# Hybrid encoder step on one core: square sums of the input norm regrouped, pooled products from split operands, two last chunks on GpSimd

## The chip, the cores and the metric

One core of one Trainium2 chip runs the program. The metric is device time in microseconds (us). Before the change three runs gave 808.74, 809.33 and 810.02 us; the median, 809.33 us, is the time before. One more execution was profiled: it took 807.98 us, and its span from the first to the last instruction is 806.0 us.

## The reference, cut to what matters

The reference computes one layer for 16 meta rows, 512 prompt rows and 64 sample rows (592 rows of 1024 numbers). All of it is float32. The parts that the change touches:

```
hp = layer_norm(concat(meta, x_prompt), ln_in_g, ln_in_b); hs = layer_norm(x_sample, ...)   # input norm
z = h @ w_in + b_in                      # split into u, q, k, v, ga, gb
pooled = trailing means of u over 2, 4, 8, 16 rows, minus u      # one window for each group of 128 columns
pool_out = einsum('btgc,gcd->btgd', pooled, w_pool_grp) * pool_scale   # four 128x128 products
attn = stick_breaking_attention(q, keys, vals)
mix = sigmoid(ga) * (pool_out @ w_br_pool) + sigmoid(gb) * (attn @ w_br_attn)
h = layer_norm(ALPHA * h + mix @ w_out + b_out)
f = square(relu(h @ w_mlp1 + b_mlp1)) @ w_mlp2 + b_mlp2
y = layer_norm(ALPHA * h + f, ln2_g, ln2_b)              # last norm, then the output
```

## The kernel before, in words

Activations stand transposed: 128 features on the partitions, eight chunks (k = 0 to 7) for the 1024 features, and the rows along the free axis, in two halves of 296 columns in the first stage. A float32 product is mostly made as three float32r products: each operand x is split into hi = x rounded to float32r and lo = x - hi, and TensorE adds hi*hi, lo*hi and hi*lo in PSUM. ScalarE makes the hi parts and VectorE the lo parts, of weights (units of 128x1024 from one stream) and of activations. Where a product is small it is left as a plain float32 matmul, which the trace shows as two instructions.

Each engine runs its own list of instructions in written order; semaphores tie the lists together. Nothing is reordered at run time, so an instruction that waits holds everything behind it on its engine.

**Input norm and keys (0 to 50 us).** x arrives in eight transfers. TensorE sums the columns with matrices of 1/1024 (`half1_sum`, `square_sum`), VectorE subtracts the mean (`centre0`), ScalarE squares (`square0`) and takes the inverse root (`root0`, a Ln, an Exp and a Square) and VectorE finishes it (`inverse0`). Then, chunk by chunk: VectorE scales (`scale0`, line 1953), ScalarE adds the bias and rounds (`norm0_hi`, line 1282), VectorE makes the rest (`norm0_lo`, line 1959), and TensorE multiplies the chunk into two key units at a time (`keys_pair`, lines 737 to 740): the second unit of the pair runs `lag` chunks behind the first, and an optional function is called between chunks. There are four such passes: units 0, 1 and units 2, 3 on the first half of the columns (half 0), then both pairs on half 1. In the first pass the lag is 1 and after each chunk one square sum of half 1 is taken (line 706); in the three others the lag is 4. Weights of units 2 and 3 are split inside this stage (`split_keys`, lines 1288 and 1966). The results leave PSUM by `key_out` on ScalarE (line 1295), and the next pass waits for that: unit 1 on half 1 needs the bank that `key_out(3, 0)` frees.

**Attention and fillers (75 to 300 us).** Eleven items of attention. In each TensorE makes scores, ScalarE and VectorE turn them into softplus sums and split these (`sums_hi`, `sums_lo`, the latter line 2063), TensorE takes suffix sums (line 866), ScalarE exponentiates, TensorE multiplies by the values. While TensorE waits for the softplus sums it does halves of linear units from the stream. GpSimd meanwhile makes the pooled frames (lines 2660 to 2671, until 176 us) and then issues a small store. The four products of the pooled prompt frames with `w_pool_grp` (`pool_group`, line 937) are plain float32 matmuls of 512 columns, after items 6, 7 and 8 and inside item 9; VectorE scales each (`pool_scale`) back into `u_t`. A fifth call does the 64 sample columns.

**Last norm (780 to 806 us).** The columns are in two parts of 320 and 256. For the second part, after the last product, ScalarE, VectorE and TensorE make the mean and the inverse root (lines 1758 to 1769, 2503 to 2522), VectorE and GpSimd centre four chunks each (lines 2513, 2752), then for k = 0 to 7 VectorE scales (`scale2`, line 2533), ScalarE adds the bias (`norm2_out`, line 1775), and the SP queue stores chunks 0-1, 2-3, 4-5, 6 and 7 as they are ready (line 605). The kernel ends when the stores have landed.

Of the kernel before, what the change touches and what calls it, by code (L numbers as in the profile page):

```python
# [5 lines left out]
F32 = mybir.dt.float32  # L6
F32R = mybir.dt.float32r
BF16 = mybir.dt.bfloat16
ALU = mybir.AluOpType
# [147 lines left out]
def encoder_step(nc, x, wstream, w2_d, vecs_d, bv_d, kc_d, vc_d, state_d, wpool_d, y_out, k_out, v_out, s_out):  # L157
    with ExitStack() as ctx:
# [47 lines left out]


# [95 lines left out]
        win_done, ust_done, pooled = sem("win_done"), sem("ust_done"), sem("pooled")  # L303
        pool_mm, pool_scaled, pool_hi_done, pool_lo_done = (
# [27 lines left out]
        n2_last_mean = sem("n2_last_mean")  # L332
# [90 lines left out]
        BY_DVE2 = (4, 4)  # L423

# [118 lines left out]
        def _(sp):  # L543
# [56 lines left out]
            for p, c in enumerate(PARTS2):  # L600

                for ks in ([slice(k, k + 2) for k in range(0, KC - 2, 2)] + [slice(k, k + 1) for k in range(KC - 2, KC)]
                           if p == LAST2 else [slice(k, k + 1) for k in range(KC)]):
                    sp.wait_ge(n2_out, KC * p + ks.stop)
                    sp.dma_start(y_out[:, ks, c], r2[:, ks, c]).then_inc(y_stored, 16)
            sp.wait_ge(y_stored, 16 * (2 * KC - 3))
# [6 lines left out]
        def _(pe):  # L613
# [154 lines left out]


            keys_pair(0, 0, square_sum1, 1)  # L770
            keys_pair(2, 0)
            keys_pair(0, 1)
# [156 lines left out]
            def pool_group(s):  # L929

                pe.wait_ge(pooled, 1)
                pe.wait_ge(wpool_in, 16)
# [3 lines left out]
                if s < 4:  # L936
                    pe.matmul(small[:, :], wpool[:, s, :], u_t[:, s, META:UP], start=True, stop=True)\
                        .then_inc(pool_mm, 1)
# [238 lines left out]
        def _(act):  # L1177
# [127 lines left out]
            root0(0)  # L1305
            act.wait_ge(vecs_in, 16)
            norm0_hi(0, 0)
            for k in range(1, KC):
                norm0_hi(k, 0)
                square0(k - 1, 1)  # L1310
                if k in (4, 6):
                    split_keys(k // 2)
            square0(7, 1)
            key_out(0, 0)
            root0(1)
            key_out(1, 0)
# [486 lines left out]
            for k in range(KC):  # L1803
                norm2_out(k, LAST2)


        @block.vector
        def _(dve):
# [168 lines left out]
            for k in range(1, KC):  # L1977
                scale0(k, 0)
                norm0_lo(k - 1, 0)
                centre0(k - 1, 1)  # L1980
            norm0_lo(7, 0)
            centre0(7, 1)

            dve.wait_ge(lo_split, 2)
            split_keys(2)
            split_keys(3)
            inverse0(1)
# [587 lines left out]
            for k in range(KC):  # L2575
                scale2(k, LAST2)

        @block.gpsimd
        def _(pool):
# [114 lines left out]
            pool.wait_ge(pooled, 1)  # L2694
# [117 lines left out]
```

## Time and profile before

| | |
|---|---|
| median of three runs | 809.33 us |
| profiled execution | 807.98 us, span 806.0 us |
| TensorE busy | 793.0 us (98% of the span) |
| VectorE busy | 506.4 us (63%) |
| ScalarE busy | 392.3 us (49%) |
| GpSimd busy | 101.8 us (13%) |
| chain of waits | TensorE 97%, ScalarE 1%, VectorE 1%, transfers 1% |

A timeline row gives the start in us from the span's beginning, the duration, the engine (PE is TensorE, DVE VectorE, ACT ScalarE, POOL GpSimd, SP the queue that issues transfers), the line of the kernel, the operation, output<-inputs with shapes, the count where neighbours of one kind are merged, and in brackets the idle time before it and who ended it. Matmuls overlap, so their spacing and not their duration is their price. Rows of the windows view give a stretch, its length, each engine's busy time and instruction count, the TensorE clock as a share, the share of the transfer engines and GB/s.

### The profile page before, as it was taken

What the parts mean: (1) busy time and instruction counts of PE and PEld (TensorE: products, weight loads), DVE (VectorE), ACT (ScalarE), POOL (GpSimd) and SP (SyncE); (2) the same over time, 40 slices, a digit from 0 to 9 for tenths busy, and PEclk for the clock granted to TensorE, in tenths of its full rate; (3) what the DMA queues carried; (4) which work ended last, traced back from release to release, by engine and by line L of the source; (5) the groups of instructions that cost most, each with busy time, mean ns of one, the idle gap of its engine ahead of it and who ended that gap; (6) DMA issues with size and microseconds to landing.
All of it is one profiled execution on the core that took longest, in us unless ns stands there. A gap on an engine that the chain in (4) does not pass through costs nothing.

```text
span 806.0 us, 14543 instructions
## 1 busy us (share of the span) xinstructions
PE 793.0 (98%) x5880; PEld 765.2 (95%) x5880; DVE 506.4 (63%) x858; ACT 392.3 (49%) x654; POOL 101.8 (13%) x120
## 2 busy tenths in 40 slices
PE   8999999999999999999999999999999999999995
PEld 6999899998988999999999999999999999999994
DVE  5823444753536376876877779775667887445645
ACT  4623345654646475562556663334554433344324
POOL 2100000570000000007720000000000000000355
PEclk9999999999999999999999999999999999999998
DMA  8732131112111112243302214222221423222203
GB/s 297 264 130 97 53 113 53 54 56 79 53 54 53 53 58 74 79 131 106 92 14 79 66 39 158 79 105 79 82 72 55 157 79 105 80 78 80 79 1 117
DMA packets 23033, 71.61 MB, mean 89 GB/s; under 512 B 2416, under 2 KB 6656, under 8 KB 22592
## 3 DMA queue, kind: packets, MB, share of 16 engines
q1 hardware_dynamic: 22288, 68.23, 25.7%
q0 software_dynamic: 544, 2.52, 0.9%
q8 instruction: 40, 0.66, 0.3%
q14 instruction: 17, 0.14, 0.1%
q10 hardware_dynamic: 144, 0.07, 0.1%
HBM read 65.96 MB, written 4.85 MB: 88 GB/s over the span
## 4 chain that ended last, share of the span: by engine, by line
PE 97%; ACT 1%; DVE 1%; DMA 1%; issue 0%; SPq 0%; ACTq 0%; DVEq 0%
PE lin L620 15%; PE lin L621 15%; PE lin L622 15%; PE z L1093 6%; PE z L1095 5%; PE z L1096 5%; PE z L866 3%; PE lin L996 3%; PE lin L997 3%; PE lin L998 3%; PE lin L1114 2%; PE lin L1113 2%; PE lin L1112 2%; PE z L925 1%; PE lin L740 1%; PE lin L737 1%
## 5 line engine op out<-in xcount | busy, mean ns | idle before, releaser
L620 PE MATMUL lin<-h_hi,whi 128*128 128x288 f32 (+1 forms) x832 | 247.3, 297 | 0.0
L621 PE MATMUL lin<-h_lo,whi 128*128 128x288 f32 (+1 forms) x832 | 245.9, 296 | 0.0
L622 PE MATMUL lin<-h_hi,wlo 128*128 128x288 f32 (+1 forms) x832 | 245.0, 294 | 0.0
L622 PEld LDWEIGHTS lin<-h_hi,wlo 128*128 128x128 f32 x832 | 156.6, 188 | 0.0
L620 PEld LDWEIGHTS lin<-h_hi,whi 128*128 128x128 f32 x832 | 156.5, 188 | 0.1
L621 PEld LDWEIGHTS lin<-h_lo,whi 128*128 128x128 f32 x832 | 156.4, 188 | 0.1
L1815 DVE TENSOR_TENSOR wlo<-raw,whi 128x1024 fp32r<-128x1024 f32 x65 | 80.3, 1235 | 34.8 <-ACT whi L1187 30.0
L1187 ACT ACTIVATE whi<-raw 128x1024 fp32r<-128x1024 f32 x58 | 60.9, 1051 | 50.3 <-PE lin L622 32.4
L1605 ACT ACTIVATE relu_t<-lin,vecs 128x288 f32<-128x288 f32 x60 | 30.1, 501 | 91.4 <-PE lin L622 88.0
L2257 DVE TENSOR_TENSOR relu_sq<-relu_t 128x288 f32<-128x288 f32 x60 | 27.5, 458 | 64.4 <-ACT relu_t L1605 64.4
L1093 PE MATMUL z<-f_ops,whi 128*128 128x288 f32 x216 | 64.0, 296 | 0.0
L1095 PE MATMUL z<-f_ops,whi 128*128 128x288 f32 x216 | 63.3, 293 | 0.0
L1096 PE MATMUL z<-f_ops,wlo 128*128 128x288 f32 x216 | 63.2, 293 | 0.0
L1652 ACT ACTIVATE whi<-w_set 128x768 fp32r<-128x768 f32 x36 | 30.5, 846 | 52.0 <-PE z L1096 41.7
L2732 POOL TENSOR_TENSOR sum<-r 128x576 f32<-128x576 f32 x1 | 1.4, 1435 | 346.4 <-DVE r L2497 346.4
L1093 PEld LDWEIGHTS z<-f_ops,whi 128*128 128x128 f32 x216 | 40.6, 188 | 0.4 <-issue 0.4
L2404 DVE TENSOR_TENSOR wlo<-w_set,whi 128x768 fp32r<-128x768 f32 x36 | 34.5, 957 | 9.9 <-ACT whi L1652 9.8
L1096 PEld LDWEIGHTS z<-f_ops,wlo 128*128 128x128 f32 x216 | 40.6, 188 | 0.0
L1095 PEld LDWEIGHTS z<-f_ops,whi 128*128 128x128 f32 x216 | 40.5, 188 | 0.0
L2034 DVE SCALAR_TENSOR_TENSOR sa<-z,sa 128x512 f32<-128x512 f32 (+4 forms) x25 | 19.8, 794 | 26.8 <-ACT sa L1363 26.8
L1095 PE MATMUL z<-f_ops,third_hi 128*128 128x288 f32 x120 | 35.6, 297 | 0.0
L1096 PE MATMUL z<-f_ops,third_lo 128*128 128x288 f32 x120 | 35.4, 295 | 0.0
(348 smaller groups left out, 1900.3 us busy)
## 6 DMA issues: line engine op xcount, KB each, us to landing
raw<-w_stream SPq DMA_DIRECT2D x88, 512.0 KB, 3.5
w_set<-w_sets SPq DMA_DIRECT2D x32, 384.0 KB, 3.6
r<-x_t SPq DMA_DIRECT2D x8, 296.0 KB, 5.1
kcache<-k_cache SPq DMA_DIRECT2D x1, 2048.0 KB, 9.0
vcache<-v_cache SPq DMA_DIRECT2D x1, 2048.0 KB, 10.7
y<-r SPq DMA_DIRECT2D x8, 160.0 KB, 1.8
k_new<-k_t POOLq DMA_DIRECT2D x1, 1184.0 KB, 4.8
v_new<-v_t POOLq DMA_DIRECT2D x1, 1024.0 KB, 5.2
```

The costliest lines, as they stand in the source:

```text
L620: pe.matmul(out, w_h, hi, start=first, stop=False)
L621: pe.matmul(out, w_h, lo, start=False, stop=False)
L622: return pe.matmul(out, w_l, hi, start=False, stop=last)
L1093: pe.matmul(out, w_h, f_op(f, i, 0), start=opens and i == 0, stop=False, skip_group_check=True)
L1095: pe.matmul(out, w_h, f_op(f, i, 1), start=False, stop=False, skip_group_check=True)
L1096: last = pe.matmul(out, w_l, f_op(f, i, 0), start=False, stop=i == PRS - 1, skip_group_check=True)
L1187: nc.scalar.activation(whi[:, j % SPLIT, :], raw[:, j, :], ACT.Copy).then_inc(hi_split, 1)
L1605: nc.scalar.activation(dst, lin[:, bank, 0:HA], ACT.Relu, bias=vec(V_B1 + u)).then_inc(bank_free[bank], 1)
L1652: nc.scalar.activation(op_home(o)[0], w_set[g % 2][:, i, :], ACT.Copy).then_inc(s_hi, 1)
L1815: tt(wlo[:, j % SPLIT, :], raw[:, j, :], whi[:, j % SPLIT, :].bitcast(F32), ALU.subtract)\
L2257: tt(dst, src, src, ALU.mult).then_inc(f_sq_done, 1)
L2404: tt(home[1], w_set[g % 2][:, RAW_SLOT[q], :], home[0].bitcast(F32), ALU.subtract).then_inc(s_lo, 1)
```

## The change

Three separate edits:

- **Input norm.** ScalarE's and VectorE's lists are reordered: in the first pass they no longer centre and square half 1 between the chunks of half 0; units 2 and 3 are split at other places; centring and squaring come afterwards, in two batches on VectorE. TensorE takes the eight square sums in the second pass, two after chunk 2 and six after chunk 3 of unit 2, with unit 3 a full eight chunks behind. In the third pass the lag is 2 instead of 4.
- **Pooled products.** GpSimd splits `w_pool_grp` (one pair of instructions on 512 columns) and each of the four pooled groups (a pair on 512 columns each) into hi and lo; the lo parts take the place of the frames. The rounding of groups 2 and 3 waits for the products of groups 0 and 1, because `u_hi` has two slots. TensorE's float32 matmul becomes three float32r ones.
- **Last chunks.** VectorE copies the inverse root from PSUM to SBUF and then scales only chunks 0 to 5; GpSimd scales chunks 6 and 7 and applies weight and bias. SP stores 0-1, 2-3 and 6-7; ScalarE issues the store of 4-5 itself.

```diff
 PE
-            keys_pair(0, 0, square_sum1, 1)
-            keys_pair(2, 0)
-            keys_pair(0, 1)
+            def square_sums1(k):
+                for n in {1: (0, 1), 2: range(2, KC)}.get(k, ()):
+                    square_sum1(n)
+            keys_pair(0, 0, None, 1)
+            keys_pair(2, 0, square_sums1, KC)
+            keys_pair(0, 1, None, 2)
             keys_pair(2, 1)
...
-                pe.wait_ge(pooled, 1)
-                pe.wait_ge(wpool_in, 16)
+                pe.wait_ge(wp_lo_done, 1)
...
-                    pe.matmul(small[:, :], wpool[:, s, :], u_t[:, s, META:UP], start=True, stop=True)\
-                        .then_inc(pool_mm, 1)
+                    pe.wait_ge(u_lo_done, s + 1)
+                    hi, lo = u_hi[:, s % 2, :], u_lo[:, s, META:UP]
+                    pe.matmul(small[:, :], wp_hi[:, s, :], hi, start=True, stop=False)
+                    pe.matmul(small[:, :], wp_lo[:, s, :], hi, start=False, stop=False)
+                    pe.matmul(small[:, :], wp_hi[:, s, :], lo, start=False, stop=True).then_inc(pool_mm, 1)
 ACT
             root0(0)
+            split_keys(2)
             act.wait_ge(vecs_in, 16)
-            norm0_hi(0, 0)
-            for k in range(1, KC):
+            for k in range(KC):
                 norm0_hi(k, 0)
-                square0(k - 1, 1)
-                if k in (4, 6):
-                    split_keys(k // 2)
-            square0(7, 1)
+            split_keys(3)
             key_out(0, 0)
+            for k in range(2):
+                square0(k, 1)
+            key_out(1, 0)
+            for k in range(2, KC):
+                square0(k, 1)
             root0(1)
-            key_out(1, 0)
...
-            for k in range(KC):
+            for k in range(G_FROM2):
                 norm2_out(k, LAST2)
+            act.wait_ge(n2_out, KC * LAST2 + G_FROM2)
+            act.dma_start(y_out[:, G_FROM2 - 2:G_FROM2, PARTS2[LAST2]], r2[:, G_FROM2 - 2:G_FROM2, PARTS2[LAST2]])\
+                .then_inc(y_stored, 16)
 DVE
                 scale0(k, 0)
                 norm0_lo(k - 1, 0)
-                centre0(k - 1, 1)
             norm0_lo(7, 0)
-            centre0(7, 1)
             dve.wait_ge(lo_split, 2)
             split_keys(2)
+            for k in range(4):
+                centre0(k, 1)
             split_keys(3)
+            for k in range(4, KC):
+                centre0(k, 1)
             inverse0(1)
...
-            for k in range(KC):
+            nc.vector.tensor_scalar(rstd2[:, PARTS2[LAST2]], r2_rstd(LAST2), 1.0, None, ALU.mult)\
+                .then_inc(n2_rstd_copy, 1)
+            for k in range(G_FROM2):
                 scale2(k, LAST2)
 POOL
             pool.wait_ge(pooled, 1)
+            pool.wait_ge(wpool_in, 16)
+            pool.wait_ge(qk_done, 3)
+            nc.gpsimd.tensor_scalar(wp_hi[:, :, :], wpool[:, :, :], 1.0, 0.0, ALU.mult, ALU.add).then_inc(wp_hi_done, 1)
+            pool.wait_ge(wp_hi_done, 1)
+            nc.gpsimd.tensor_tensor(wp_lo[:, :, :], wpool[:, :, :], wp_hi[:, :, :].bitcast(F32), ALU.subtract)\
+                .then_inc(wp_lo_done, 1)
+            for s in range(4):
+                if s >= 2:
+                    pool.wait_ge(pool_mm, s - 1)
+                nc.gpsimd.tensor_scalar(u_hi[:, s % 2, :], u_t[:, s, META:UP], 1.0, 0.0, ALU.mult, ALU.add)\
+                    .then_inc(u_hi_done, 1)
+                pool.wait_ge(u_hi_done, s + 1)
+                nc.gpsimd.tensor_tensor(u_lo[:, s, META:UP], u_t[:, s, META:UP], u_hi[:, s % 2, :].bitcast(F32),
+                                        ALU.subtract).then_inc(u_lo_done, 1)
...
             centre2(LAST2)
+            pool.wait_ge(n2_rstd_copy, 1)
+            for k in range(G_FROM2, KC):
+                c = PARTS2[LAST2]
+                pool.wait_ge(n2_centred_g, KC * LAST2 - sum(BY_DVE2) + k + 1)
+                nc.gpsimd.tensor_tensor(r2[:, k, c], r2[:, k, c], rstd2[:, c], ALU.mult).then_inc(n2_scaled_g, 1)
+                pool.wait_ge(n2_scaled_g, k - G_FROM2 + 1)
+                nc.gpsimd.tensor_scalar(r2[:, k, c], r2[:, k, c], vec(V_LN2_G + k), vec(V_LN2_B + k), ALU.mult, ALU.add)\
+                    .then_inc(n2_out_g, 1)
 SP (last part of the columns)
-                for ks in ([slice(k, k + 2) for k in range(0, KC - 2, 2)] + [slice(k, k + 1) for k in range(KC - 2, KC)]
-                           if p == LAST2 else [slice(k, k + 1) for k in range(KC)]):
-                    sp.wait_ge(n2_out, KC * p + ks.stop)
-                    sp.dma_start(y_out[:, ks, c], r2[:, ks, c]).then_inc(y_stored, 16)
+            for k in (0, 2, G_FROM2):
+                if k < G_FROM2:
+                    sp.wait_ge(n2_out, KC * LAST2 + k + 2)
+                else:
+                    sp.wait_ge(n2_out_g, KC - G_FROM2)
+                sp.dma_start(y_out[:, k:k + 2, PARTS2[LAST2]], r2[:, k:k + 2, PARTS2[LAST2]]).then_inc(y_stored, 16)
```

## Rows read from the trace of the kernel before

**Rows 1.** Page, section 1: busy us, share of the span, instructions.

```profile
PE 793.0 (98%) x5880; PEld 765.2 (95%) x5880; DVE 506.4 (63%) x858; ACT 392.3 (49%) x654; POOL 101.8 (13%) x120
```

**Rows 2.** Timeline, TensorE, pass of units 2, 3 and start of half 1.

```profile
31.86 0.37 PE L737 MATMUL lin<-h_hi,k_hi 128*128 128x296 f32 x1
...
36.40 0.30 PE L737 MATMUL lin<-h_hi,whi 128*128 128x296 f32 x1
```

**Rows 3.** Timeline, VectorE and ScalarE, 17 to 36 us, in two lists.

```profile
17.71 0.53 DVE L1959 SCALAR_TENSOR_TENSOR h_lo<-r,vecs,h_hi 128x296 fp32r<-128x296 f32 x1 [0.24 <-ACT h_hi L1282]
...
27.86 2.35 DVE L1966 TENSOR_TENSOR k_lo<-raw,k_hi 128x1024 fp32r<-128x1024 f32 x2
...
34.42 0.52 DVE L1959 SCALAR_TENSOR_TENSOR h_lo<-r,vecs,h_hi 128x296 fp32r<-128x296 f32 x1
34.86 0.52 DVE L1953 SCALAR_TENSOR_TENSOR r<-r,vecs,small 128x296 f32<-128x296 f32 x1
...
17.14 0.97 ACT L1282 ACTIVATE h_hi<-r,vecs 128x296 fp32r<-128x296 f32 x2 [1.67 <-DVE r L1953]
...
29.89 0.51 ACT L1273 ACTIVATE rstd<-z,eps 128x296 f32<-128x296 f32 x1 [1.06 <-PE z L706]
...
31.27 0.49 ACT L1295 ACTIVATE k_t<-lin,vecs 128x296 f32<-128x296 f32 x1
...
34.97 0.99 ACT L1282 ACTIVATE h_hi<-r,vecs 128x296 fp32r<-128x296 f32 x2
```

**Rows 4.** Chain of waits: start us, us added to the chain, what, count.

```profile
29.35 0.50 PE z L706 x2
...
80.86 0.24 PE small L791
...
222.39 1.06 PE small L937 x2
```

**Rows 5.** Timeline, GpSimd, VectorE, TensorE, 150 to 187 us, in three lists.

```profile
152.33 0.70 POOL L2665 TENSOR_SCALAR win<-win 128x591 f32<-128x591 f32 x1
...
169.43 1.19 POOL L2660 TENSOR_TENSOR win<-win 128x600 f32<-128x600 f32 x1
...
175.97 0.62 POOL L2678 DMA_DIRECT2D state_new<-ust  x1
...
170.27 1.43 DVE L1815 TENSOR_TENSOR wlo<-raw,whi 128x1024 fp32r<-128x1024 f32 x1 [0.63 <-ACT whi L1187]
...
176.17 0.99 DVE L2029 TENSOR_TENSOR sa<-sa 128x800 f32<-128x800 f32 x1
177.08 0.98 DVE L2063 TENSOR_TENSOR sp_lo<-sa,sp_hi 128x800 fp32r<-128x800 f32 x1
178.29 1.23 DVE L2063 TENSOR_TENSOR sp_lo<-sa,sp_hi 128x1024 fp32r<-128x1024 f32 x1 [0.23 <-ACT sp_hi L1395]
...
181.46 0.68 DVE L2121 TENSOR_TENSOR q_lo<-q_t,q_hi 128x512 fp32r<-128x512 f32 x1
...
178.48 0.34 PE L866 MATMUL z<-sp_hi,tri_r 128*128 128x400 f32 x1
...
179.71 0.39 PE L866 MATMUL z<-sp_hi,tri_r 128*128 128x512 f32 x1
...
186.30 0.39 PE L847 MATMUL z<-q_hi,k_hi 64*128 64x272 f32 x2
```

**Rows 6.** Timeline, the last norm's second part, 796 to 804 us.

```profile
796.87 2.77 POOL L2752 TENSOR_TENSOR r<-r,mean 128x256 f32<-128x256 f32 x4 [3.31 <-ACT mean L1759]
797.10 0.43 DVE L2506 TENSOR_SCALAR z<-z 128x256 f32<-128x256 f32 x1
...
800.33 3.30 ACT L1775 ACTIVATE r<-r,vecs 128x256 f32<-128x256 f32 x8 [1.48 <-DVE r L2533]
```

**Rows 7.** Windows of 0.2 us in the last stores; columns as told above.

```profile
802.80:803.00 0.20, 0.00 (x0) 0.00 (x0) 0.20 (x1) 0.20 (x2) 0.00 (x0) 0.50 0.53 174
...
805.00:805.20 0.20, 0.00 (x0) 0.00 (x0) 0.00 (x0) 0.00 (x0) 0.00 (x0) 0.50 0.93 323
```

More of the change, by code:

```diff
@@ L204, in encoder_step @@
         inv_d = sb("inv_d", [P], F32, A0 + 32832)
+        u_hi = sb("u_hi", [2, SEQ], F32R, A0 + 31480)
+        u_lo = sb("u_lo", [4, UT], F32R, A0 + 23360)
+        wp_hi, wp_lo = sb("wp_hi", [4, P], F32R, 17664), sb("wp_lo", [4, P], F32R, A0 + 13632)
         KQ = 3 * P
@@ L303, in encoder_step @@
         win_done, ust_done, pooled = sem("win_done"), sem("ust_done"), sem("pooled")
+        wp_hi_done, wp_lo_done, u_hi_done, u_lo_done = (
+            sem("wp_hi_done"), sem("wp_lo_done"), sem("u_hi_done"), sem("u_lo_done"))
         pool_mm, pool_scaled, pool_hi_done, pool_lo_done = (
@@ L331, in encoder_step @@
         n2_sq, n2_sum, n2_sumsq = ([sem(f"{n}{p}") for p in range(2)] for n in ("n2_sq", "n2_sum", "n2_sumsq"))
-        n2_last_mean = sem("n2_last_mean")
+        n2_last_mean, n2_rstd_copy, n2_scaled_g, n2_out_g = (
+            sem("n2_last_mean"), sem("n2_rstd_copy"), sem("n2_scaled_g"), sem("n2_out_g"))
         n2_msq, n2_mean, n2_var, n2_guess, n2_rstd = (
@@ L423, in encoder_step @@
         BY_DVE2 = (4, 4)
+        G_FROM2 = 6
         SUMMED2 = (KC, KC - 1)
@@ L599, in _ @@
                         load_unit(q4, j)
-            for p, c in enumerate(PARTS2):
-                for ks in ([slice(k, k + 2) for k in range(0, KC - 2, 2)] + [slice(k, k + 1) for k in range(KC - 2, KC)]
-                           if p == LAST2 else [slice(k, k + 1) for k in range(KC)]):
-                    sp.wait_ge(n2_out, KC * p + ks.stop)
-                    sp.dma_start(y_out[:, ks, c], r2[:, ks, c]).then_inc(y_stored, 16)
-            sp.wait_ge(y_stored, 16 * (2 * KC - 3))
+            for k in range(KC):
+                sp.wait_ge(n2_out, k + 1)
+                sp.dma_start(y_out[:, k, PARTS2[0]], r2[:, k, PARTS2[0]]).then_inc(y_stored, 16)
+            for k in (0, 2, G_FROM2):
[4 more added lines that the diff above has]
+                sp.dma_start(y_out[:, k:k + 2, PARTS2[LAST2]], r2[:, k:k + 2, PARTS2[LAST2]]).then_inc(y_stored, 16)
+            sp.wait_ge(y_stored, 16 * (KC + 4))
             sp.wait_ge(k_stored, 16)
@@ L1305, in _ @@
             root0(0)
+            split_keys(2)
             act.wait_ge(vecs_in, 16)
-            norm0_hi(0, 0)
-            for k in range(1, KC):
+            for k in range(KC):
                 norm0_hi(k, 0)
-                square0(k - 1, 1)
-                if k in (4, 6):
-                    split_keys(k // 2)
-            square0(7, 1)
+            split_keys(3)
             key_out(0, 0)
+            for k in range(2):
[3 more added lines that the diff above has]
+                square0(k, 1)
             root0(1)
-            key_out(1, 0)
             norm0_hi(0, 1)
```

## The prediction, made before the changed kernel ran

> **What bounds the kernel now.** I read the busy shares first: TensorE is busy 793.0 of 806.0 us [rows 1]. Nearly all of the 13 us that it is not lie at the two ends, before the first keys and in the last norm's tail. So the middle is paid by TensorE's work alone: what is taken off its list there shortens the time one to one, as long as no other engine becomes late for it, and a wait put into it lengthens the time one to one. At the two ends the waits count instead. So the timelines of the three places decide, and in each the reader should look for the operation that TensorE (or the last store) would wait for, and how long before its use it is ready.
>
> **The change, part by part.**
>
> **Input norm.** TensorE's own work is the same: 96 matmuls of 296 columns on half 0 and eight square sums at 0.50 us [rows 4]. Between 31.86 and 36.40 lie 33 matmuls, 0.137 us each [rows 2]. Only waits can go. Now the first pass is paced by TensorE with the square sums between the chunks, after a start that VectorE holds up. The last square sum ends at 29.85 (29.35 + 0.50) [rows 4], and half 1 starts at 36.40 [rows 2].
>
> After the change VectorE has only scale and rest for each chunk, 0.44 us apart between 34.42 and 34.86 [rows 3], 0.87 a chunk. The first rest still starts at 17.71 [rows 3]. Six chunks on is 22.93; the eighth rest waits for ScalarE's rounding and starts near 23.6. Then comes the lo split of unit 2: two of them took 2.35 [rows 3], so one ends about 1.2 after its start at 24.05, at 25.3. TensorE, which has 6 x 0.137 = 0.82 of work a chunk, follows VectorE's pace of 0.87 and is done at the same moment. So unit 2 starts at 25.3 and its first result is there 0.4 later (a matmul that restarts takes 0.37, [rows 2]), at 25.7; eleven more and eight square sums (11 x 0.137 + 8 x 0.50 = 5.5) end at 31.2. The squares themselves are in time: VectorE and ScalarE need until about 29.9 for the last. From 31.2, 36 matmuls (4.9) lead to half 1, at 36.1 where the end of the matmul before 36.40 was 36.56. That is 0.4 us gained. It costs nothing that ScalarE splits unit 2 ahead of the first rounding: it is idle there for 1.67 us before 17.14 [rows 3], and a split on it takes about 1.
>
> Then it is given back. Half 1's chain hangs on the last square sum, which now ends 1.35 later while TensorE has 0.4 less to do before it wants half 1. In the profile the root starts at 29.89, the scale of chunk 3 at 34.86, 5.0 after the sum [rows 3]. ScalarE rounds chunk 3 some 0.55 after that and can start the next operation 0.43 later, since a pair of roundings takes 0.99 [rows 3]. That next one is the eviction of unit 3, which frees the bank of unit 1; it takes 0.49 [rows 3]. It ends 6.5 after the last sum, and TensorE's first result on that bank comes 0.47 later (eviction at 31.27 + 0.49, next matmul 31.86 + 0.37) [rows 2, 3], at 6.95. With lag 2 TensorE wants that bank after 36 + 9 matmuls, so the 46th would end 46 x 0.137 = 6.3 after the sum. The wait is 0.65; behind it stand the rest of both units and everything after. Nothing later in half 1 waits. Net: 0.65 - 0.4 = **0.2 us lost**. Bounds: 0.4 gained if that eviction comes in time, 0.5 lost if the square sums also end some 0.3 late.
>
> **Pooled products.** A float32 product of 512 columns costs 1.06 us on the chain (one of four such rows) [rows 4]. A float32r one of 512 columns costs 0.24 [rows 4], three 0.71. Four groups: 4 x 0.35 = 1.4 us less for TensorE. The operands are ready long before: products start at 222, GpSimd is free from 176.
>
> But GpSimd's new work is not free at its start. GpSimd's store issue ends at 175.97 + 0.62 = 176.59 [rows 5], where VectorE is making the lo parts of item 4's softplus sums. Those are needed at once: the two end at 178.06 and 179.52, and TensorE uses them at 178.48 and 179.71 [rows 5], 0.4 and 0.2 us later. Where GpSimd and a VectorE operation with two inputs in SBUF meet, one stands still: a GpSimd addition runs from 169.43 to 170.62, and the VectorE subtraction of 1024 columns that starts at 170.27 ends at 171.70, taking 1.43 where the same shape takes 1.23 [rows 5]. It ended 1.08 after GpSimd: its own length less 0.15. With that, and taking turns: VectorE's sum holds until 177.16; the rounding (0.70 for 591 columns [rows 5], 0.61 for 512) ends at 177.62; the first lo part (0.98) ends at 178.45, just in time; the subtraction (1.19 for 600 columns, 1.02 for 512) ends at 179.32; the second lo part ends at 180.40, not 179.52. TensorE wants it at 179.71 and restarts about 0.1 late: **0.8 us of waiting**. Bounds: none, if VectorE keeps its place, and 1.4 if each blocked operation starts from nothing. Nothing makes up for it, since TensorE has no idle time afterwards. Net 1.4 - 0.8 = **0.6 us gained**, between 1.4 gained and nothing.
>
> The Trainium skill, page "SBUF — State Buffer", section "SBUF: two separate sides", says that the port pair which VectorE and GpSimd share is an exclusive lock for a whole instruction, and that the loser blocks fully. By that rule nothing overlaps, the 0.15 goes, the two lo parts end at 178.75 and 181.0, TensorE loses about 1.4, and the whole change comes out at 0.4 us slower instead of 0.2 faster; that lies inside the forecast's own range, and the 170.27 row speaks for the small overlap.
>
> The pairs for groups 2 and 3 run behind the products of groups 0 and 1, near 223 and 238, with more than 20 us to spare and no softplus work beside them. The fill of `ones_r` behind them moves by 60 us and is not needed before the output product near 300.
>
> **Last chunks.** VectorE's copy (0.43 for the like of it [rows 6], a little less in step) delays chunk 0's scale, ScalarE's output and the first store by 0.4. ScalarE writes six chunks, not eight, at 0.40 each (3.30 for eight with overlap [rows 6]), so its last output comes 0.8 - 0.4 = 0.4 earlier. GpSimd's four instructions at no more than 0.69 each (2.77 for four [rows 6]) from 800.2 end by 803.0, and its store is out before the transfers of 0-3 are through. If issue set the end, 0.4 would be gained. But the transfers do: from the first packet to 805.2 the engines are full (0.93 and more) save for two gaps of about a tenth, one at 802.8 [rows 7]. A megabyte that starts 0.4 later and at best closes the gaps ends **0.2 us later**. Bounds: 0.4 gained, 0.4 lost.
>
> **Sum.** +0.2 - 0.6 + 0.2 = -0.2 us on the profiled execution's 807.98, so 807.8. The median of the runs stands 1.35 above that execution; with it the forecast is **809.1 us**. Changes below 0.2% (1.6 us) can't be told from none with this kernel.
>
> **The rivals.**
>
> *No collision (chance 0.20).* GpSimd's first subtraction falls beside ScalarE's part or VectorE keeps the port, and the 1.4 stays whole: -1.4 + 0.2 + 0.2 = -1.0, 808.3 us. For it: the slack and the collision are both tenths of a microsecond. Against it: GpSimd is free at exactly the wrong time, and the 170.27 row shows VectorE losing.
>
> *All three pay (0.15).* No collision, no wait for the eviction in half 1 (the 0.4 stays), and the last store sets the end (another 0.4): -2.2, 807.1 us. For it: ScalarE's list does end earlier. Against it: each needs a row read the other way.
>
> *The collision goes on (0.08), the slower side.* GpSimd has four more instructions before it must wait, and VectorE then owes the lo split of a weight unit, `k_lo` and `q_lo`; `q_lo` ends at 182.14 and item 5's scores use it at 186.30 [rows 5]. With 0.9 lost already and four turns (two of 0.46, two of 0.87, together 2.7) it ends at 185.7, against scores moved to 187.1. It decides from 4.1 us of loss on; every further microsecond is one of the kernel, and with turns twice as long TensorE loses about 2: 811.0 us.
>
> *The three products cost what one did (0.07).* Weight loads that show would eat the 0.35 a group; then only the losses stay: +1.2, 810.5 us. Against it: rows of three float32r products in a row at 0.24.
>
> **How the numbers follow.** The forecast's own case has 0.50, with its own range of 808.4 to 809.9. Faster by over 0.2%: the 0.15 and a little of the first rival, 0.19. Slower: 0.08 and a little of the last, 0.10. The rest, 0.71, is no change. The range reaches from the middle of the all-pay case to the edge of the collision that goes on: 807.3 to 810.3.
>
> **What would show it.** Right: a wait of TensorE of about 0.65 before the first matmul of unit 1 on half 1, with the eviction of unit 3 just before it; VectorE's 1024-column lo part near 179 ending some 0.9 later than now against TensorE's list, and TensorE idle there; three float32r matmuls per group in 0.71; full transfer engines until the end. Wrong: TensorE without idle time between 20 and 790 us, a gain at the start that lasts to 50 us, or a gap in the transfers before the last store.

## The result, and the profile after

The changed kernel takes 810.11 us (median of 22 runs, 808.87 to 812.40); the kernel before took 809.28 us in the 22 runs beside them. The ratio, which is not that of the two medians (they lie 0.83 apart), is 1.0013 with a 95% interval of 1.0007 to 1.0019: 1.05 us slower, 0.6 to 1.5. The forecast was 0.2 us faster. The profiled execution took 808.87 us, span 807.1 us. One run of all that are told of below, 858.31 us at a granted clock of 0.849 with the best version, is a slow one and left out of ratios and spreads.

The busy times hardly show it. TensorE's share, from the page of the changed kernel:

```profile
PE 792.2 (98%) x5883; PEld 764.7 (95%) x5884; DVE 509.3 (63%) x857; ACT 391.6 (49%) x652; POOL 115.7 (14%) x134
```

It has 0.8 us less to do than before [rows 1] in a span 1.1 us longer. So it waits more, and the question is where. I set each product of TensorE against the same product in the trace of before; the table gives the start after minus the start before, in us, at some times of the trace of before. A step between two columns is a gain or a loss in that stretch.

| | first key product | 50 | 170 | 200 | 275 | 362 | 375 | 480 | 600 | 700 | 785 |
|---|---|---|---|---|---|---|---|---|---|---|---|
| changed kernel | -0.23 | 0.0 | 0.0 | 1.62 | 0.98 | 0.98 | 1.50 | 1.47 | 0.87 | 0.87 | 0.87 |

Six steps: the execution reached its first key product 0.23 earlier; +0.23 in the input norm; +1.62 between 176 and 182; -0.64 at the four pooled products; +0.52 at 367; -0.60 between 495 and 550. The last one is not the change's: further down it is in half of the kernels, whatever they hold.

*Input norm.* The timeline of the changed kernel where unit 1 begins on half 1, TensorE's products and the eviction of unit 3 on ScalarE:

```profile
36.69 0.30 PE L752 MATMUL lin<-h_hi,wlo 128*128 128x296 f32 x1
...
37.04 0.40 PE L754 MATMUL lin<-h_lo,whi 128*128 128x296 f32 x1
...
37.62 0.38 PE L751 MATMUL lin<-h_hi,whi 128*128 128x296 f32 x1 [0.18 <-issue]
...
37.03 0.49 ACT L1316 ACTIVATE k_t<-lin,vecs 128x296 f32<-128x296 f32 x1
```

Products here are 0.137 us apart [rows 2]. Between the first two rows it is 0.35, so 0.21 of waiting (the low part of chunk 2), and between the next two 0.58, so 0.44 (the bank that the eviction frees): 0.65 in all, against 0.43 gained at the start of half 1. That start is 18.15 us after the first key product, 35.74 - 17.59, where it was 36.40 - 17.82 = 18.58 [rows 2]; 35.74, 17.59 and 17.82 are starts of TensorE's products in the two traces.

*Collision.* GpSimd, VectorE and TensorE of the changed kernel where GpSimd begins to split:

```profile
176.63 1.42 POOL L2728 TENSOR_SCALAR wp_hi<-wpool 128x512 fp32r<-128x512 f32 x1
...
178.13 1.90 POOL L2730 TENSOR_TENSOR wp_lo<-wpool,wp_hi 128x512 fp32r<-128x512 f32 x1
...
180.01 1.59 POOL L2735 TENSOR_SCALAR u_hi<-u_t 128x512 fp32r<-128x512 f32 x1
...
181.68 2.15 POOL L2738 TENSOR_TENSOR u_lo<-u_t,u_hi 128x512 fp32r<-128x512 f32 x1
...
176.16 1.41 DVE L2056 TENSOR_TENSOR sa<-sa 128x800 f32<-128x800 f32 x1
...
177.50 1.39 DVE L2090 TENSOR_TENSOR sp_lo<-sa,sp_hi 128x800 fp32r<-128x800 f32 x1
...
178.81 2.30 DVE L2090 TENSOR_TENSOR sp_lo<-sa,sp_hi 128x1024 fp32r<-128x1024 f32 x1
...
181.47 1.21 DVE L1840 TENSOR_TENSOR wlo<-raw,whi 128x1024 fp32r<-128x1024 f32 x1
...
182.60 1.65 DVE L2145 TENSOR_TENSOR k_lo<-k_t,k_hi 128x384 fp32r<-128x384 f32 x1
...
184.17 1.09 DVE L2148 TENSOR_TENSOR q_lo<-q_t,q_hi 128x512 fp32r<-128x512 f32 x1
...
178.94 0.45 PE L885 MATMUL z<-sp_hi,tri_r 128*128 128x400 f32 x1 [0.31 <-DVE sp_lo L2090]
...
181.17 0.51 PE L885 MATMUL z<-sp_hi,tri_r 128*128 128x512 f32 x1 [0.73 <-DVE sp_lo L2090]
```

Before, VectorE's sum took 0.99, its two low parts 0.98 and 1.23, `q_lo` 0.68 [rows 5]; they take 1.41, 1.39, 2.30 and 1.09 now. GpSimd's operations are stretched as well: the same rounding takes 0.62 and the same subtraction 1.09 to 1.29 where nothing is beside them. TensorE's first suffix sum starts 0.46 later than at 178.48 [rows 5] (0.31 of it idle), for the first low part, and the one that was at 179.71 [rows 5] starts 1.46 later (0.73 idle), for the second: scores of item 5 come 1.61 late. `k_lo` and `q_lo` are late too, but scores at 187.91 don't wait for them.

The ends of these rows show in what way. From the rounding on, GpSimd and the VectorE operations with two inputs in SBUF take strict turns: each ends its own unhindered length, less 0.14, after the end of the other engine's operation before it. The rounding ends at 178.05 = 177.57 + 0.62 - 0.14; the first low part at 178.89 = 178.05 + 0.98 - 0.14; the subtraction, 1.29 long alone, at 180.03; the second low part at 181.11; and so on to `q_lo` at 185.26, each within 0.02. VectorE's weight split keeps its length (1.21), since its turn came as it began; GpSimd's subtraction beside it, begun at 181.68, takes 2.15. Only the first of the rows stands outside this: the sum began 0.47 before GpSimd's rounding and took 0.42 more than alone all the same. Why, no run shows.

*Products.* The first pooled group on TensorE and the first score behind it:

```profile
223.94 0.50 PE L957 MATMUL small<-u_hi,wp_hi 128*128 128x512 f32 x1
...
224.28 0.39 PE L958 MATMUL small<-u_hi,wp_lo 128*128 128x512 f32 x1
...
224.51 0.40 PE L959 MATMUL small<-u_lo,wp_hi 128*128 128x512 f32 x1
...
224.84 0.39 PE L866 MATMUL z<-q_hi,k_hi 64*128 64x272 f32 x2
```

The group now occupies 224.84 - 223.94 = 0.90, where the float32 one occupied 1.06 [rows 4]: 0.16 gained. The other three gain 0.15 to 0.17 each, and together that is the step of 0.64.

*Middle norm at 367 us.* In neither list did the change touch this place. Before, on VectorE and GpSimd, the split of a weight unit of the output product and GpSimd's first sum of the middle norm:

```profile
360.55 1.22 DVE L1830 TENSOR_TENSOR stay_lo<-raw,stay_hi 128x1024 fp32r<-128x1024 f32 x1
...
360.78 1.66 POOL L2705 TENSOR_TENSOR sum<-r 128x288 f32<-128x288 f32 x1 [183.97 <-DVE r L2210]
```

After, GpSimd, VectorE and TensorE:

```profile
361.41 0.81 POOL L2750 TENSOR_TENSOR sum<-r 128x288 f32<-128x288 f32 x1 [119.64 <-DVE r L2237]
...
361.54 1.76 DVE L1855 TENSOR_TENSOR stay_lo<-raw,stay_hi 128x1024 fp32r<-128x1024 f32 x1
...
368.14 0.37 PE L1017 MATMUL lin<-mix_hi,stay_hi 128*128 128x288 f32 x1 [0.28 <-DVE r L2226]
```

GpSimd's sum has the same releaser, VectorE's addition, which ends at 360.27 and 361.26. Before, it began 0.51 later and ran into VectorE's split, taking 1.66 while the split took its usual 1.22. After, it begins 0.15 later, ahead of the split: it takes 0.81 and the split 1.76. The turns explain both lengths: whoever began first keeps its own (1.22, 0.81), and the other ends its own length less 0.14 behind (361.77 + 0.81 - 0.14 = 362.44; 362.22 + 1.22 - 0.14 = 363.30). VectorE's eviction that follows is late by as much, and TensorE stands for a bank at 368.14.

*Last chunks.* VectorE's copy and scales, ScalarE's outputs and SP's stores, then the transfers (the last two columns are the busy share of the transfer engines and GB/s):

```profile
800.68 0.42 DVE L2603 TENSOR_SCALAR rstd<-small 128x256 f32<-128x256 f32 x1
...
801.02 2.43 DVE L2560 SCALAR_TENSOR_TENSOR r<-r,vecs,small 128x256 f32<-128x256 f32 x6
...
801.53 2.50 ACT L1797 ACTIVATE r<-r,vecs 128x256 f32<-128x256 f32 x6 [1.81 <-DVE r L2560]
...
802.46 1.87 SPq L619 DMA_DIRECT2D y<-r  x3
```

```profile
803.00:804.00 1.00, 0.00 (x0) 0.00 (x0) 0.45 (x2) 1.00 (x3) 0.82 (x2) 0.50 0.65 231
...
804.00:805.00 1.00, 0.00 (x0) 0.00 (x0) 0.00 (x0) 0.03 (x1) 0.00 (x0) 0.50 0.94 323
...
805.00:806.00 1.00, 0.00 (x0) 0.00 (x0) 0.00 (x0) 0.00 (x0) 0.00 (x0) 0.50 1.08 381
...
806.00:807.00 1.00, 0.00 (x0) 0.00 (x0) 0.00 (x0) 0.00 (x0) 0.00 (x0) 0.50 0.33 114
```

The copy takes 0.42 and puts off VectorE's scales, and with them the first store, by 0.34 against TensorE's last products. The transfer engines are nearly full from 804 to 806 (0.94 and 1.08), as they were at 805.00 before [rows 7]: the delay reaches the end, save for 0.1 that a closed gap gives back: windows of 0.2 us have two gaps in the transfers before, at 802.8 [rows 7] and 803.6, and one now, at 804.0.

### The profile page after: what moved, and what is told of

It reads as the page before. It is cut to its first block, busy times and chain, and to the rows that moved or that the text cites. A ratio compares the mean times of both kernels' runs of the same rounds, so it can differ in the third digit from the quotient of the medians.

```text
span 807.1 us, 14560 instructions
## 1 busy us (share of the span) xinstructions
PE 792.2 (98%) x5883; PEld 764.7 (95%) x5884; DVE 509.3 (63%) x857; ACT 391.6 (49%) x652; POOL 115.7 (14%) x134
## 4 chain that ended last, share of the span: by engine, by line
PE 93%; DVE 3%; ACT 2%; issue 1%; DMA 1%; SPq 0%; DVEq 0%; ACTq 0%
PE lin L634 15%; PE lin L635 14%; PE lin L636 14%; PE z L1114 6%; PE z L1116 5%; PE z L1117 5%; PE z L885 3%; PE lin L1017 3%; PE lin L1018 2%; PE lin L1019 2%; PE lin L1134 2%; PE lin L1133 2%; PE lin L1135 2%; PE z L944 1%; PE z L636 1%
```

## The experiments

Times are ratios to runs of the kernel before on the same chip, with 95% intervals, and in brackets what they are in us. The profiled executions give the same table as above (TensorE's starts minus those of the kernel before):

| kernel | first key | 50 | 170 | 200 | 275 | 362 | 375 | 480 | 600 | 700 |
|---|---|---|---|---|---|---|---|---|---|---|
| input norm alone | -0.35 | 1.16 | 1.18 | 1.18 | 1.18 | 1.18 | 1.19 | 1.18 | 1.19 | 1.78 |
| products alone | -0.05 | 1.14 | 1.14 | 2.75 | 2.11 | 2.11 | 2.64 | 2.63 | 2.03 | 2.01 |
| last chunks alone | 2.10 | 3.47 | 3.48 | 3.49 | 3.48 | 3.49 | 3.49 | 3.48 | 2.91 | 2.91 |
| late splitting | -0.07 | -0.07 | -0.07 | -0.06 | -0.70 | -0.70 | -0.19 | -0.20 | -0.19 | 0.41 |
| late splitting, again | 0.05 | 1.43 | 1.42 | 1.43 | 0.78 | 0.77 | 1.30 | 1.27 | 0.66 | 0.65 |
| splitting without its use | -0.35 | -0.34 | -0.32 | 1.28 | 1.28 | 1.30 | 1.82 | 1.78 | 1.18 | 1.17 |
| fills instead of splitting | 0.15 | 1.57 | 1.58 | 1.59 | 1.59 | 1.58 | 2.11 | 2.09 | 1.49 | 1.48 |
| late splitting and sum | 1.91 | 3.25 | 3.26 | 3.27 | 2.62 | 2.63 | 2.63 | 2.63 | 2.64 | 3.23 |
| the same, again | -0.28 | -0.29 | -0.28 | -0.28 | -0.92 | -0.91 | -0.91 | -0.92 | -0.91 | -0.31 |
| input norm, early eviction | 0.23 | 0.26 | 0.26 | 0.26 | 0.26 | 0.26 | 0.26 | 0.26 | 0.27 | 0.87 |
| that and late splitting, sum | 0.61 | 0.65 | 0.66 | 0.66 | 0.02 | 0.02 | 0.03 | 0.02 | 0.03 | 0.63 |
| whole change, two waits | 0.52 | 2.01 | 2.02 | 2.02 | 1.38 | 1.37 | 1.38 | 1.37 | 0.79 | 0.78 |

Three things in it go with the execution and not with the kernel, and they have to be taken out before two rows are compared: the first column (the start); a step of 1.2 to 1.4 before 50, in seven rows (TensorE's clock, last section; where the input norm's regrouping is in too, its 0.23 comes on top); and a step of 0.6 either between 480 and 600 or between 600 and 700 (the pace of two long stretches). One kernel run twice, the late splitting, has them differently in its two rows, and all else to 0.03 the same.

**The three parts alone.** The change's diff, cut to the part:

```diff
# e1: PE keys_pair and square_sums1, ACT and DVE lists of the input norm; products, tail as before
# e2: GpSimd's splitting and the three float32r products; input norm, tail as before
# e3: copy, scale2 for k < 6, GpSimd's chunks 6 and 7, stores; all else as before
```

> The input norm's part alone. Theory (the input norm came out as forecast): 0.2 us slower than before, TensorE waits about 0.4 to 0.6 for the bank of the third unit before the first matmul of unit 1 on half 1, and the first q unit starts 0.2 later relative to the first key matmul. Rival (the regrouping is worth nothing either way, and the 0.23 of the whole change's trace was scatter of the start): 0.0, no such wait. Rival (it gains): 0.4 faster.

> The pooled products' part alone. Theory (collision 1.6, saving 0.15 for each of four groups = 0.6): 1.0 us slower than before; VectorE's two low parts of the sums of item 4 end at about 178.9 and 181.1 and TensorE is idle about 0.3 and 0.7 before its suffix sums. Rival (as forecast: collision 0.8, saving 1.4): 0.6 faster. Rival (the collision came from the input norm's shift of the relative times of GpSimd and TensorE, and goes away when GpSimd's frames keep their old time): 0.6 faster too, but with no idle time at the suffix sums.

> The last chunks' part alone. Theory (transfers set the end, first store 0.4 later, gaps partly closed): 0.2 us slower than before. Rival (ScalarE's shorter list sets the end): 0.4 faster. Rival (nothing of it shows): 0.0. A trace that is equal to the one of before until 795 us.

Input norm: 1.0002, 0.9993 to 1.0010 (+0.2, -0.6 to 0.8). Its trace has the same two waits before unit 1 on half 1, 0.35 and 0.58 between the same products. Products: 1.0018, 1.0009 to 1.0026 (+1.5, 0.7 to 2.1), with TensorE idle 0.31 and 0.73 for `sp_lo` as in the changed kernel, and steps of +1.61, -0.64 and +0.53, 1.50 in all. The collision is the same whether the input norm is regrouped or not, so the reading by the input norm's shift falls, and so does the forecast's. Last chunks: 1.0005, 0.9992 to 1.0017 (+0.4, -0.6 to 1.4); its trace shows no step of its own up to 785. For the first and the last part the interval holds 0.0 and 0.2 alike; what speaks for 0.2 there are the traces. From TensorE's last product with `r` (795.40 before) to the end of the span the three kernels with the new last chunks need 10.87 or 10.88 us in their traces, the eleven with the old ones 10.63 or 10.64.

**Late splitting.** GpSimd waits until VectorE has nothing urgent:

```diff
             pool.wait_ge(qk_done, 3)
+            pool.wait_ge(kq_lo_done, 4)
             nc.gpsimd.tensor_scalar(wp_hi[:, :, :], wpool[:, :, :], 1.0, 0.0, ALU.mult, ALU.add)
```

> The pooled products' part alone, with one wait more: GpSimd starts its splitting only after VectorE has made the low parts of item 4's sums and then of k and q (about 182.2 us), when nothing that VectorE makes is wanted soon. Theory (collision 1.6, saving 0.6): 0.6 us faster than before, VectorE's low parts as long as before (0.99, 1.23), four groups still 0.7 each. Rival (saving 0.35 for each group, as the prediction had it): 1.4 faster. Rival (the collision only moves to the next softplus sums, near 187 to 190): 0.0 to 0.5 slower, with VectorE's subtractions of item 5 stretched.

> The late splitting without the wait before GpSimd's first sum of the middle norm, again, beside the two below. Theory (saving 0.64, of which 0.5 is given back at 366 us): 0.1 to 0.2 us faster than before; the trace has GpSimd's sum 0.15 us after its releaser, VectorE's weight split behind it at 1.76, and TensorE idle at 366 us. Rival (the first measurement of 0.65 faster was right and nothing is given back): 0.6 to 0.7 faster.

0.9992, 0.9982 to 1.0002, and again 0.9994, 0.9984 to 1.0004 (-0.6, -1.5 to +0.2, and -0.5, -1.3 to +0.3). VectorE, GpSimd and TensorE of the first of the two:

```profile
177.01 0.99 DVE L2072 TENSOR_TENSOR sp_lo<-sa,sp_hi 128x800 fp32r<-128x800 f32 x1
...
178.22 1.23 DVE L2072 TENSOR_TENSOR sp_lo<-sa,sp_hi 128x1024 fp32r<-128x1024 f32 x1 [0.23 <-ACT sp_hi L1404]
...
185.82 1.83 DVE L1824 TENSOR_TENSOR wlo<-raw,whi 128x1024 fp32r<-128x1024 f32 x1 [0.64 <-ACT whi L1196]
...
182.64 0.61 POOL L2708 TENSOR_SCALAR wp_hi<-wpool 128x512 fp32r<-128x512 f32 x1 [6.11 <-DVE q_lo L2130]
...
366.46 0.37 PE L1005 MATMUL lin<-mix_hi,stay_hi 128*128 128x288 f32 x1 [0.28 <-DVE r L2208]
```

The low parts have their old lengths, the +1.61 is gone, and the products keep their -0.64. GpSimd's work still stretches a VectorE operation, the weight split at 185.82 (1.83 instead of 1.22), but TensorE doesn't wait for that one: a collision costs what hangs on the operation that loses. Both runs' traces have the idle 0.28 at 366.46 or 1.47 later, and both rows of the table the step of 0.5 there, so 0.5 of the 0.64 is given back. I had not expected that when the first of the two ran.

**Splitting without its use, and fills instead of it.** The first keeps GpSimd's new work but leaves TensorE its float32 product; the second has GpSimd write 512 columns twelve times at the same moment, without an SBUF operand to read:

```diff
 # e5, on the products' part
-                    pe.matmul(small[:, :], wp_hi[:, s, :], hi, start=True, stop=False)
-                    pe.matmul(small[:, :], wp_lo[:, s, :], hi, start=False, stop=False)
-                    pe.matmul(small[:, :], wp_hi[:, s, :], lo, start=False, stop=True).then_inc(pool_mm, 1)
+                    pe.matmul(small[:, :], wpool[:, s, :], u_t[:, s, META:UP], start=True, stop=True)
 # e6, on the kernel before
             pool.wait_ge(pooled, 1)
+            for n in range(12):
+                nc.gpsimd.memset(win[:, 0, 0:512], 0.0).then_inc(win_done, 1)
+                pool.wait_ge(win_done, done + n + 1)
```

> GpSimd does all of its splitting as in the changed kernel, but TensorE goes on multiplying the float32 operands, so that the new work stands alone without what it was to buy; head and tail as before. Theory (collision 1.6, saving of the products 0.15 a group): TensorE is 1.6 us later than before from item 5's scores on, and stays at 1.6 until 360 us, where the products alone gave back 0.64; there a wait of 0.3 to 0.5 comes (GpSimd's first sum of the middle norm starts earlier than before and VectorE's weight split behind it is late). In all 2.1 us slower than before (1.6 without that wait). Rival (the products save 0.35 a group, the collision costs more than I read): 2.4 to 2.9 slower, the difference to the kernel with the products being 1.4.

> The kernel before, with twelve fills of 512 columns on GpSimd where the change has its splitting (behind the store issue at 176.6): GpSimd is busy beside the same VectorE operations, but reads nothing from SBUF. Theory (GpSimd's reads of SBUF operands are what holds VectorE up): VectorE's low parts take 0.99 and 1.23 as before, 0.0 us. Rival (any GpSimd instruction that runs at that time holds VectorE up): the low parts are stretched, up to 1.6 slower.

Splitting alone: 1.0024, 1.0013 to 1.0034 (+1.9, 1.1 to 2.8). TensorE is 1.6 late from 200 and stays so to 362; beside "products alone", which falls by 0.64 there, this is the saving of the products by itself. The first group there, TensorE:

```profile
223.60 1.13 PE L944 MATMUL small<-u_t,wpool 128*128 128x512 f32 x2
...
224.66 0.40 PE L854 MATMUL z<-q_hi,k_hi 64*128 64x272 f32 x2
```

It occupies 1.06 as before. Fills: 0.9996, 0.9986 to 1.0005 (-0.3, -1.1 to +0.4). GpSimd and VectorE, and GpSimd's sum of the middle norm:

```profile
178.19 6.98 POOL L2696 MEMSET win<- 128x512 f32 x12
...
177.75 0.99 DVE L2029 TENSOR_TENSOR sa<-sa 128x800 f32<-128x800 f32 x1
...
178.66 0.99 DVE L2063 TENSOR_TENSOR sp_lo<-sa,sp_hi 128x800 fp32r<-128x800 f32 x1
...
179.87 1.23 DVE L2063 TENSOR_TENSOR sp_lo<-sa,sp_hi 128x1024 fp32r<-128x1024 f32 x1 [0.23 <-ACT sp_hi L1395]
...
362.01 0.80 POOL L2708 TENSOR_TENSOR sum<-r 128x288 f32<-128x288 f32 x1 [176.57 <-DVE r L2210]
```

GpSimd is busy from 0.44 into the sum to the end of both low parts, and they take 0.99, 0.99 and 1.23: nothing is stretched. So it is not GpSimd's being busy, nor its writing, but, as far as these two kinds of work go, its reading of SBUF operands beside a VectorE operation with two of them. The Trainium skill, page "SBUF — State Buffer", section "SBUF: two separate sides", says this too: against a VectorE operation with two SBUF inputs only a GpSimd operation that reads SBUF counts. The same section of the Trainium skill says that whichever starts first gets the port pair for its whole instruction and that the other blocks fully. The turns of the changed kernel agree with that, less the 0.14 by which the next one's own length reaches into the one before; the first pair doesn't, since VectorE's sum began 0.47 ahead of GpSimd's rounding and took 1.41 all the same.

The last row has a second result: GpSimd's first sum of the middle norm begins early (0.80 long) and TensorE loses 0.53 at 367 with the fills too, though their row has no step at 200 or 275. So the loss there follows from GpSimd's having had more to do behind its frames, and neither from the splitting as such nor from TensorE's being early.

**Late splitting and late sum.** On top of the late splitting, GpSimd's first sum of the middle norm starts behind ScalarE's first square:

```diff
+                if m == 1 and h == 0:
+                    pool.wait_ge(n1_sq, 1)
                 nc.gpsimd.tensor_tensor(sum1[:, c], r1[:, 0, c] if m == 1 else sum1[:, c], r1[:, m, c], ALU.add)
```

> Late splitting as in the run before with that name, and GpSimd's first sum of the middle norm waits for ScalarE's first square too (some 0.45 us). Theory (0.5 of the saving was given back at 366 us, because GpSimd's sum got in ahead of VectorE's split of a weight unit, which took 1.76 instead of 1.22): that split takes 1.2 again, TensorE has no idle time at 366 us, and its lead on the kernel before stays at 0.6 to 0.7 from 270 to 495 us; 0.6 to 0.7 faster than before, 0.5 faster than without the wait. Rival (VectorE was the limit there anyway, by its own work): the same idle time at 366 us, lead 0.2 afterwards, 0.1 to 0.2 faster than before.

> The late splitting with that wait, again: the first measurement (2.2 us faster) is more than its trace accounts for (0.64 of lead on the kernel before, kept past 366 us). Theory (the rest, 1.5, was chance: executions differ by TensorE's clock in the first keys, by their start and by the pace of two long stretches, all of it without regard to the change): 0.6 to 0.7 faster than before. Rival (the kernel has something that the one profiled execution doesn't show): about 2 faster again.

The mechanism came out in both: VectorE and GpSimd of the second run,

```profile
359.64 1.22 DVE L1839 TENSOR_TENSOR stay_lo<-raw,stay_hi 128x1024 fp32r<-128x1024 f32 x1
...
360.01 1.51 POOL L2732 TENSOR_TENSOR sum<-r 128x288 f32<-128x288 f32 x1 [120.14 <-ACT sq L1550]
```

the split takes 1.22, TensorE has no idle time at 366 us, and in both rows the lead of 0.64 is the same at 275 and at 480. The times don't agree: 0.9972, 0.9962 to 0.9983 (-2.3, -3.1 to -1.4), and then, for the same program on another chip, 0.9997, 0.9986 to 1.0009 (-0.2, -1.1 to +0.7). The lead of 0.64 that both traces show lies in the second interval and not in the first, so I take the first to have missed; but its trace is of its slowest run, 810.99, where the other eight lie between 806.55 and 807.52, and what made those fast is not shown. Runs of one kernel differ by 2.0 to 4.5 us from the fastest to the slowest; when that goes together within one set, its interval can miss. The mean of the two is -1.25 us.

**Input norm with the earlier eviction, alone and in the best version.**

```diff
             norm0_hi(2, 1)
-            norm0_hi(3, 1)
             key_out(3, 0)
+            norm0_hi(3, 1)
```

> The input norm's part alone, with ScalarE's eviction of unit 3 put ahead of the rounding of chunk 3 on half 1. Theory (the 0.4 gained at the start of half 1 is given back by the wait for that eviction's bank): no wait at unit 1 of half 1, TensorE's first q unit 0.2 to 0.4 earlier after its first key product than before; 0.2 us faster than before, 0.4 faster than the part as it stands. Rival (chunk 3 is then the late one): TensorE waits as long for the rounded chunk 3, no difference to the part as it stands, 0.2 slower than before.

> Late splitting with that wait, and the input norm's regrouping with the earlier eviction; the last chunks as before. Theory (0.64 from the products, 0.0 from the input norm, since VectorE's pace of 0.87 a chunk takes back what half 1 starts earlier): as the run above, 0.6 to 0.7 faster than before. Rival (the input norm's 0.2 counts once more): 0.8 to 0.9 faster.

Alone: 0.9996, 0.9984 to 1.0009 (-0.3, -1.3 to +0.7). From first key product to 50 its row moves by +0.03, where the part as it stands has +0.23 (in the changed kernel's row): 0.2 better, not 0.4. TensorE and VectorE there:

```profile
37.51 0.40 PE L740 MATMUL lin<-h_lo,whi 128*128 128x296 f32 x1
...
38.43 0.35 PE L740 MATMUL lin<-h_lo,whi 128*128 128x296 f32 x1
...
36.93 0.52 DVE L1965 SCALAR_TENSOR_TENSOR h_lo<-r,vecs,h_hi 128x296 fp32r<-128x296 f32 x1
...
37.80 0.52 DVE L1965 SCALAR_TENSOR_TENSOR h_lo<-r,vecs,h_hi 128x296 fp32r<-128x296 f32 x1
```

The bank is free in time, and now VectorE's pace of 0.87 a chunk (37.80 - 36.93) shows: TensorE waits 0.21 at 37.51 for the low part of chunk 2 and a few hundredths at each chunk after it. So what half 1 starts earlier is lost to VectorE, which finishes no sooner. The best version (this, late splitting, late sum, the old last chunks): 0.9996, 0.9987 to 1.0005 (-0.3, -1.0 to +0.4); its row has +0.04, then -0.64, and no step at 367. By the trace it and the late splitting with the late sum are 0.6 ahead of the kernel before; the runs put the best version ahead of the changed kernel (no more than +0.4 against no less than +0.6), and, but for the set with -2.3, neither clearly ahead of the kernel before.

**The whole change with the two waits.**

```diff
             pool.wait_ge(qk_done, 3)
+            pool.wait_ge(kq_lo_done, 4)
...
+                if m == 1 and h == 0:
+                    pool.wait_ge(n1_sq, 1)
```

> The whole changed kernel with the two waits on GpSimd (splitting after the low parts of k and q; first sum of the middle norm after ScalarE's first square). Theory (input norm +0.2, products -0.64, last chunks +0.2, collision 1.6 and the later 0.5 both gone): 0.2 us faster than before, where the changed kernel was 1.05 slower; against the trace of before TensorE is 0.2 later from the input norm on, 0.4 earlier after the fourth product group and still so at 490 us. Rival (more than these two places makes the changed kernel slower): 0.5 to 1 slower than before.

0.9989, 0.9979 to 0.9998 (-0.9, -1.7 to -0.2). It has no idle time of TensorE between 178 and 184 or at 367, and -0.64 at the products. Against the changed kernel's +1.05 the two waits are worth about 1.9; the trace of the changed kernel prices the two places at 1.62 + 0.52 = 2.1. Against the kernel before, the steps of the traces come to -0.4: 0.23 - 0.64 + 0.23, and 0.2 outside the span (last section). The interval holds that as it does the expected -0.2.

## Why the prediction was wrong

*Input norm, +0.2: right, by its steps.* 0.43 gained at the start of half 1 (0.4 forecast), 0.65 of waiting (0.65), although a third of the wait is for the low part of chunk 2, which the forecast did not have. When the eviction's wait is taken away, VectorE's pace takes its place.

*Products, "Four groups: 4 x 0.35 = 1.4": mis-sized.* They save 4 x 0.16 = 0.64. The 1.06 on the float32 side was the distance from the group's first matmul to the next operation, between attention products, and holds what these neighbours cost at either end; the 0.71 on the other side was three matmuls in a running row and holds none of it. In the changed kernel the first of the three takes 0.34 to the next (224.28 - 223.94) and the last 0.33, not 0.24. The forecast called the 1.06 one of four such rows, but there are three: the fourth float32 group, between a linear product and a suffix sum, stood for only 0.86 in the chain, and its three products stand for 0.71 there, so the gain is 0.15 in that place too. Both sides had to be read between the same neighbours.

*Collision, "0.8 us of waiting": mis-sized.* It was 1.6, and this is the larger error by a little. The mechanism was right: the engines take turns, each with its own length less 0.14 (0.15 in the forecast, from the one row of 170.27 [rows 5]). Two lengths put into it were wrong. The forecast let VectorE's sum hold until 177.16, since it began first, and it held until 177.57. And it took 1.02 for GpSimd's subtraction, scaled down from an addition of 600 columns, where the subtraction is 1.29 alone. Together, with a few hundredths from the overlap, these put the end of the second low part at 181.11, not 180.40; the remaining 0.1 is that the suffix sums restart more slowly than reckoned (0.34 instead of 0.22 from the first to the next). By the rule that the forecast cites from the Trainium skill, page "SBUF — State Buffer", section "SBUF: two separate sides", with the same two lengths, its estimate was 1.4: nearer, but by leaving out the overlap that the rows show, and not by the sizes that were wrong.

*What was not in it: 0.5 at 367 us.* The forecast looked for cover behind GpSimd's new work as far as `ones_r`, and found it. What GpSimd does next, 120 us later, is to race VectorE for a start within 0.3 us, and it now wins. The forecast had no term for it, and its sum put it at nothing. So the products, forecast as 0.6 gained, cost 1.62 - 0.64 + 0.52 = 1.5.

*Last chunks, +0.2: right by the trace.* From TensorE's last product with `r`, at 795.40 before and 796.27 after, the kernel's end is 0.24 further on: the span grew by 1.1, of which 0.87 is there already. The transfers did set the end; one of their two gaps closed.

*Sum.* By the trace, 0.23 + 1.62 - 0.64 + 0.52 + 0.23 = 1.96; the time outside the span is 0.2 shorter (below), which leaves 1.75. The runs gave 1.05, at most 1.5. What lies between I can't place; since executions differ by up to 4.5 us for other reasons, it may as well be chance.

The rival "no collision" failed where the row spoke against it, and "all three pay" with it, since the eviction's wait and the transfers came as forecast. "The collision goes on" was right in that `k_lo` and `q_lo` are stretched but wrong in that nothing waits. "The three products cost what one did" was half right: more than half of the saving of 0.35 a group isn't there.

## What to carry to other kernels

Before work is put on GpSimd, list what VectorE does in that window with two SBUF inputs, and what waits for each of these within a microsecond; then start the work where nothing does: here one wait on a semaphore was worth 1.6 us by the trace and cost nothing. When turns are added up, every operation in them needs its own measured length: an error in one is handed on to all behind it. Price a replaced instruction and its successor between the same neighbours, not one as a distance and the other as a stride. When a part is gained early in the program, compare the starts of the same instructions in both traces to the end: what is won at one place can be handed back 100 us further on, at a place that no line of the diff touches.

## What I had not expected of the hardware

**TensorE's clock in the first keys.** In seven of the fourteen profiled executions the granted clock falls for 3 to 4 us there. The windows of "products alone" (stretch, length, TensorE busy, granted clock, transfer share, GB/s):

```profile
16.00:18.00 2.00, 0.56 (x4) 1.00 0.63 170
...
18.00:20.00 2.00, 1.43 (x7) 0.78 1.13 408
...
20.00:22.00 2.00, 2.00 (x8) 0.50 0.94 363
...
22.00:24.00 2.00, 2.00 (x13) 0.87 1.02 418
```

A granted clock of 0.50 is the lower level, 1.2 GHz. TensorE had been idle for 1.44 us ahead of its first key product at 17.78; it was idle there as long in the executions whose clock stayed at 1.00. It costs 1.2 to 1.4 us each time, as much as all that this change does, and kernels with and without the regrouped input norm have it.

**Two paces.** From 495 to 550 and from 636 to 697 us the same products follow each other at 0.1326 or at 0.1311 us on average with no wait and the granted clock at 1.00 in both; each stretch differs by 0.6 us. What decides the pace is not known. The trace of before has the slow pace in the first and the fast one in the second.

**A start after a long idle.** GpSimd's first sum of the middle norm begins 0.51 us after its releaser in the kernel before, with the input norm alone, with the early eviction and with the last chunks alone, and 0.15 after it in every kernel in which GpSimd did more behind its frames, fills included (idle for 176.57 us there, for 183.97 in the former, for 120 with the splitting; where it was made to wait for ScalarE's square, 0.17 after that). What decides it was not tried.

**Outside the span.** The same two sets of kernels differ by 0.2 in what lies outside the span: 1.92 to 1.95 us on average over all runs of a kernel in the former, 1.72 to 1.76 in the latter. The cause was not tried.
